# First tiles behind three norms made from the unnormed input, their results multiplied by the norm's factor

## The reference

```
def rms_norm(x, g):
    xf = x.astype(jnp.float32)
    y = xf * lax.rsqrt(jnp.mean(xf * xf, axis=-1, keepdims=True) + RMS_EPS)
    return (y * g.astype(jnp.float32)).astype(x.dtype)
...
        h = rms_norm(x, norm_mix_pre[l])
        u = h @ w_in[l]
...
        x = x + rms_norm(y, norm_mix_post[l])
        h = rms_norm(x, norm_ffn_pre[l])
        gu = causal_dwconv(h @ w_ffn_up[l], ffn_conv_w[l])
        g, up = jnp.split(gu, 2, axis=-1)
        y = (jax.nn.gelu(g, approximate=True) * up) @ w_ffn_down[l]
        x = x + rms_norm(y, norm_ffn_post[l])
...
        z = rmsnorm(h, g_mix[l]) @ w_in[l]
```

## Time and profile before

| | |
|---|---|
| median of 3 runs | 1609.29 us (1606.79 to 1611.38) |
| the profiled execution, its own time | 1603.75 us |
| its span, first to last instruction | 1602.0 us |
| PE busy | 1507.7 us, 94% |
| DVE busy | 1082.2 us, 68% |
| ACT busy | 825.8 us, 52% |
| POOL busy | 376.2 us, 23% |
| mean granted TensorE clock | 0.978 of full |

### The profile page before, as it was taken

The page is one execution under the profiler, slowest core; times in us unless marked ns, Lnnn a source line. Parts: engine busy times, 40 slices in busy tenths (PEclk is TensorE's granted clock), DMA queues, the critical chain, the costliest instruction groups (busy, mean ns, idle before and its releaser), DMA issues.

```text
span 1602.0 us, 32178 instructions
## 1 busy us (share of the span) xinstructions
PE 1507.7 (94%) x11588; PEld 1380.9 (86%) x11588; DVE 1082.2 (68%) x1790; ACT 825.8 (52%) x1426; POOL 376.2 (23%) x166
## 2 busy tenths in 40 slices
PE   5998879999789999889999999999999999999998
PEld 4976669999678989889999999999999888888886
DVE  3426457778568988674678997999998544454444
ACT  3335445555455422354466556776665444444444
POOL 1210112222112301012233234221212222222221
PEclk9998999999889999999999999999999999999999
DMA  6630226555324500054645555444444566666664
GB/s 237 234 109 25 66 67 183 180 186 183 106 81 143 164 10 28 15 169 161 184 145 171 182 184 182 148 133 142 138 138 131 183 185 184 194 185 186 184 192 144
DMA packets 66231, 234.86 MB, mean 147 GB/s; under 512 B 8200, under 2 KB 9240, under 8 KB 66160
## 3 DMA queue, kind: packets, MB, share of 16 engines
q1 hardware_dynamic: 65760, 232.31, 45.9%
q0 software_dynamic: 400, 1.59, 0.3%
HBM read 232.80 MB, written 1.06 MB: 146 GB/s over the span
## 4 chain that ended last, share of the span: by engine, by line
PE 72%; DVE 15%; ACT 6%; issue 5%; POOL 1%; DMA 1%; DVEq 0%; SPq 0%; ACTq 0%; POOLq 0%
PE psum L681 35%; PE psum L1372 22%; PE psum L1338 4%; DVE big L1611 3%; DVE w_lo L523 3%; ACT w_hi L509 2%; DVE big L1601 2%; PE psum L1031 2%; DVE big L1651 2%; PE psum L664 1%; ACT big L2187 1%; PE psum L981 1%; PE psum L739 1%; PE psum L1022 1%; PE psum L853 1%
## 5 line engine op out<-in xcount | busy, mean ns | idle before, releaser
L681 PE MATMUL psum<-x_hi,w_hi 128*128 128x256 f32 (+1 forms) x2152 | 624.9, 290 | 39.2 <-DVE x_lo L1427 13.2
L523 POOL TENSOR_TENSOR w_lo<-ring,w_hi 128x1024 fp32r<-128x1024 f32 x141 | 352.7, 2501 | 1117.0 <-ACT w_hi L509 1117.0
L681 PE MATMUL psum<-x_lo,w_hi 128*128 128x256 f32 (+1 forms) x2152 | 613.8, 285 | 0.0
L681 PE MATMUL psum<-x_hi,w_lo 128*128 128x256 f32 (+1 forms) x2152 | 610.3, 284 | 0.0
L509 ACT ACTIVATE w_hi<-ring 128x1024 fp32r<-128x1024 f32 x424 | 445.5, 1051 | 92.0 <-PE psum L681 71.6
L523 DVE TENSOR_TENSOR w_lo<-ring,w_hi 128x1024 fp32r<-128x1024 f32 x283 | 352.2, 1245 | 151.1 <-ACT w_hi L509 147.4
L681 PEld LDWEIGHTS psum<-x_hi,w_hi 128*128 128x128 f32 x2152 | 410.7, 191 | 49.2 <-issue 32.0
L681 PEld LDWEIGHTS psum<-x_hi,w_lo 128*128 128x128 f32 x2152 | 413.4, 192 | 0.0
L681 PEld LDWEIGHTS psum<-x_lo,w_hi 128*128 128x128 f32 x2152 | 411.4, 191 | 1.7 <-issue 1.4
L2095 DVE TENSOR_TENSOR h_lo<-big,h_hi 128x256 fp32r<-128x256 f32 x128 | 69.1, 541 | 163.0 <-ACT h_hi L2519 163.0
L1372 PE MATMUL psum<-w_lo,h_hi 128*128 128x512 f32 x512 | 161.0, 395 | 0.0
(11 more groups left out here) (315 smaller groups left out, 1738.0 us busy)
## 6 DMA issues: line engine op xcount, KB each, us to landing
ring<-experts SPq DMA_DIRECT2D x256, 512.0 KB, 3.5
ring<-w_ffn SPq DMA_DIRECT2D x66, 512.0 KB, 3.5
ring<-w_in SPq DMA_DIRECT2D x46, 512.0 KB, 3.6
ring<-w_mid SPq DMA_DIRECT2D x24, 512.0 KB, 3.5
ring<-w_out SPq DMA_DIRECT2D x16, 512.0 KB, 3.6
ring<-w_q SPq DMA_DIRECT2D x16, 512.0 KB, 3.9
big<-w_cmp SPq DMA_DIRECT2D x8, 512.0 KB, 5.1
big<-bias_rows POOLq DMA_DIRECT2D x1, 1536.0 KB, 9.2
```

The source lines that it names most:

```text
L523: eng.tensor_tensor(w_lo[:, n % RING, :], ring[:, n % RING, :], w_hi[:, n % RING, :].bitcast(F32), ALU.subtract).then_inc(low_ready2 if n ...
L681: mm = pe.matmul(dst, w[:, slot, k * P:(k + 1) * P], x[:, k, t0:t0 + width], start=(n == 0), stop=(n == 3 * len(chunks) - 1))
```

## The change

At each of the three places the first tiles (tile 0 of `w1_in`, two of the FFN, three of `w2_in`) are multiplied with the split of x times gain, without the norm's factor: `x_hi` and `x_lo` come straight from the residual (`raw_act` and `low_raw`), before the norm's sum is known. The factor comes later. At norm 0 all results of `w1_in` are multiplied by `rms` when they leave PSUM, and only the gates, which need the normed input itself, get it (8 DVE operations behind tile 11; `gate_logits` moves from behind tile 12 to behind tile 13). At norms 2 and 4 the results of the raw tiles are multiplied in PSUM (`scale_raw`), while the further tiles take the normed input as before: it is made and split beside the raw tiles, and written over `x_hi` and `x_lo` when PE is done with these (`tiles_used`). The sums of norms 0 and 3 are made from squares that DVE first adds in pairs (`fold_pair`), 4 matmuls in place of 8; those of norms 2 and 4 stand between the matmuls of the first raw tile. At the start the meta tokens and the `first` parameters are loaded behind the kept parameters and tile 0. `low_rank` moves one tile back, behind tiles 4 to 6. Loops of PE are written out in part. The diff, cut to its core:

```
-            sp.dma_start(hx[:, :, 0:N_META], meta_t).then_inc(meta_loaded, 16)
             sp.dma_start(kept_sb[:], kept).then_inc(param_loaded, 16)
-            sp.dma_start(first_sb, first).then_inc(first_loaded, 16)
-            sp.dma_start(oh_tab[0:32, :], rel).then_inc(rel_loaded, 16)
...
+
+            load_tile(w1_in, 0, 0)
+            sp.dma_start(first_sb, first).then_inc(first_loaded, 16)
+            sp.dma_start(oh_tab[0:32, :], rel).then_inc(rel_loaded, 16)
...
-                    for t in range(BODY):
+                    for t in range(1, BODY):
                         load_tile(src, t, t)
+                        if t == 2:
+                            sp.dma_start(hx[:, :, 0:N_META], meta_t).then_inc(meta_loaded, 16)
...
+            pool.wait_ge(neg_row, 1)
+            split_low(pool, 2, None, (2,))
...
-            def norm_pe(n, width, bank):
-                for k in range(KD):
+            def norm_pe(n, width, bank, rows=0):
+                for k in range(rows):
                     norm_row(n, k, width, bank)
+                for q in range(rows // 2, 4):
+                    pe.wait_ge(norm_folded, FOLDED[n] + q - rows // 2 + 1)
+                    mm = pe.matmul(psum[:, bank, 0:width], const("ones"), sq[:, 2 * q, 0:width], start=(q == 0), stop=(q == 3))
+                    if q == 3:
+                        mm.then_inc(norm_sums, 1)
...
+            def project_raw(slot, dst, width, r, norm=None):
+
+                n = 0
+                for k in range(KD):
+                    if norm is not None and k % 2 == 0:
+                        norm_row(norm[0], k, width, norm[1])
+                        norm_row(norm[0], k + 1, width, norm[1])
+                        pe.wait_ge(raw_split, 4 * r + k // 2 + 1)
+                    for w, x in ((w_hi, x_hi), (w_hi, x_lo), (w_lo, x_hi)):
+                        mm = pe.matmul(dst, w[:, slot, k * P:(k + 1) * P], x[:, k, 0:width], start=(n == 0), stop=(n == 23))
+                        n += 1
+                return mm
...
-            with pe.Fori(0, 2) as i:
-                for k in range(BODY):
-                    in1(k, i)
-            for k in range(2 * BODY, LATE):
+            project(tile_split(pe, B_IN1), psum[:, 0, 0:TX], TX, first=X_RAW0).then_inc(tiles_used, 1)
+            norm_pe(0, TX, 6)
+            bias_row()
+            for k in range(1, BODY):
                 in1(k)
-                if k == 12:
+            for k in range(BODY, LATE):
+                in1(k)
+                if k == 13:
...
-            norm_pe(2, TX, 0)
+            project_raw(tile_split(pe, B_FFN), psum[:, 0, 0:TX], TX, 0, (2, 2)).then_inc(tiles_used, 1)
+            project_raw(tile_split(pe, B_FFN + 1), psum[:, 1, 0:TX], TX, 0).then_inc(tiles_used, 1)
...
-            norm_pe(4, T2, 1)
+            project_raw(tile_split(pe, B_IN2), psum[:, 0, 0:T2], T2, 1, (4, 3)).then_inc(tiles_used, 1)
+            for s in (1, 2):
+                project_raw(tile_split(pe, B_IN2 + s), psum[:, s, 0:T2], T2, 1).then_inc(tiles_used, 1)
...
+            def fold_pair(n, q, width):
+                dve.wait_ge(norm_squares, KD * n + 2 * q + 2)
+                dve.tensor_tensor(sq[:, 2 * q, 0:width], sq[:, 2 * q, 0:width], sq[:, 2 * q + 1, 0:width],
+                                  ALU.add).then_inc(norm_folded, 1)
...
+            def low_raw(r, q, src, gain):
+                dve.wait_ge(raw_high, 4 * r + q + 1)
+                for k in (2 * q, 2 * q + 1):
+                    ins = dve.scalar_tensor_tensor(out=x_lo[:, k, 0:src.shape[2]], in0=src[:, k, :], scalar=colv(gain, k, k + 1),
+                                                   in1=x_hi[:, k, 0:src.shape[2]].bitcast(F32), op0=ALU.mult, op1=ALU.subtract)
+                ins.then_inc(raw_split, 1)
+
+            def scale_raw(tile, bank, width):
+                dve.wait_ge(tiles_used, tile + 1)
+                dve.tensor_tensor(psum[:, bank, 0:width], psum[:, bank, 0:width], rms[:, 0:width], ALU.mult).then_inc(raw_scaled, 1)
+
+            def norm_pair(q, src, width, gain):
+                for k in (2 * q, 2 * q + 1):
+                    ins = dve.scalar_tensor_tensor(out=sq[:, k, 0:width], in0=src[:, k, :], scalar=colv(gain, k, k + 1),
+                                                   in1=rms[:, 0:width], op0=ALU.mult, op1=ALU.mult)
+                ins.then_inc(norm_part, 1)
+
+            def low_pair(s, q, width):
+                dve.wait_ge(high_part, 4 * s + q + 1)
+                dve.tensor_tensor(x_lo[:, 2 * q:2 * q + 2, 0:width], sq[:, 2 * q:2 * q + 2, 0:width],
+                                  x_hi[:, 2 * q:2 * q + 2, 0:width].bitcast(F32), ALU.subtract).then_inc(x_split, 1)
...
+                    if behind is not None and q > 0:
+                        behind(q - 1)
+                if behind is not None:
+                    behind(3)
...
+            for q in range(4):
+                dve.wait_ge(high_part, 4 * X_RAW0 + q + 1)
+                for k in (2 * q, 2 * q + 1):
+                    ins = dve.scalar_tensor_tensor(out=x_lo[:, k, 0:TX], in0=hx1[:, k, :], scalar=colv("mix_pre", k, k + 1),
+                                                   in1=x_hi[:, k, 0:TX].bitcast(F32), op0=ALU.mult, op1=ALU.subtract)
+                ins.then_inc(x_split, 1)
+                if q == 1:
+                    split_low(dve, 0)
+            for q in range(4):
+                fold_pair(0, q, TX)
+            split_low(dve, 1)
+            norm_scale(0, TX, 6)
...
-                    dve.tensor_copy(z1[:, trip(k, i), :], psum[:, k % BODY, 0:TX]).then_inc(in1_even, 1)
+                dve.wait_ge(tiles_used, trip(B_IN1 + k + 1, i))
+                dve.tensor_tensor(z1[:, trip(k, i), :], psum[:, k % BODY, 0:TX], rms[:, 0:TX],
+                                  ALU.mult).then_inc((in1_even, in1_odd)[k % 2], 1)
...
+            for k in range(KD):
+                ins = dve.scalar_tensor_tensor(out=sq[:, k, 0:TX], in0=hx1[:, k, :], scalar=colv("mix_pre", k, k + 1),
+                                               in1=rms[:, 0:TX], op0=ALU.mult, op1=ALU.mult)
+                if k % 2:
+                    ins.then_inc(norm_part, 1)
...
-            norm_post(1, y1, lambda q: y1[:, 2 * q:2 * q + 2, :], TX, 4, "mix_post")
-            norm_pre(2, hx1, TX, 0, "ffn_pre")
-            low_norm(X_NORM2, TX)
+            norm_post(1, y1, lambda q: y1[:, 2 * q:2 * q + 2, :], TX, 4, "mix_post", lambda q: low_raw(0, q, hx1, "ffn_pre"))
+            split_low(dve, B_FFN + 2)
+            norm_scale(2, TX, 2)
+            norm_pair(0, hx1, TX, "ffn_pre")
+            norm_pair(1, hx1, TX, "ffn_pre")
+            scale_raw(B_FFN, 0, TX)
+            low_pair(X_NORM2, 0, TX)
+            norm_pair(2, hx1, TX, "ffn_pre")
+            low_pair(X_NORM2, 1, TX)
+            norm_pair(3, hx1, TX, "ffn_pre")
+            low_pair(X_NORM2, 2, TX)
+            low_pair(X_NORM2, 3, TX)
+            scale_raw(B_FFN + 1, 1, TX)
...
-            norm_post(3, y1, ffn_y, TX, 0, "ffn_post")
+            for q in range(4):
+                fold_pair(3, q, TX)
+            norm_post(3, y1, ffn_y, TX, 0, "ffn_post", lambda q: low_raw(1, q, hx, "mix2"))
             dve.tensor_scalar(stay, colv("mu"), -1.0, 1.0, ALU.mult, ALU.add)
 
-            norm_pre(4, hx, T2, 1, "mix2")
-            low_norm(X_NORM4, T2)
...
             low(2)
+            norm_scale(4, T2, 3)
+            scale_raw(B_IN2, 0, T2)
+            norm_pair(0, hx, T2, "mix2")
             shift(0)
-            low(3)
+            scale_raw(B_IN2 + 1, 1, T2)
+            norm_pair(1, hx, T2, "mix2")
             shift(1)
+            norm_pair(2, hx, T2, "mix2")
+            norm_pair(3, hx, T2, "mix2")
+            for q in range(4):
+                low_pair(X_NORM4, q, T2)
             low(4)
+            scale_raw(B_IN2 + 2, 2, T2)
             shift(2)
             low(5)
             shift(3)
+            low(6)
+            shift(4)
             dve.wait_ge(up_ready, 4)
             step(dve.tensor_scalar(logdec, logdec, -float(np.exp(-0.5)), None, ALU.mult))
-            low(6)
-            shift(4)
...
+            def raw_act(r, src, gain, ready):
+
+                for q in range(4):
+                    ready(q)
+                    for k in (2 * q, 2 * q + 1):
+                        ins = act.activation(x_hi[:, k, 0:src.shape[2]], src[:, k, :], ACT.Copy, scale=colv(gain, k, k + 1))
+                    ins.then_inc(raw_high, 1)
+                    act.activation(sq[:, 2 * q:2 * q + 2, 0:src.shape[2]], src[:, 2 * q:2 * q + 2], ACT.Square).then_inc(norm_squares, 2)
...
+            for k in range(KD):
+                ins = act.activation(x_hi[:, k, 0:TX], hx1[:, k, :], ACT.Copy, scale=colv("mix_pre", k, k + 1))
+                if k % 2:
+                    ins.then_inc(high_part, 1)
+                if k == 3:
+                    split_high(act, 0)
             norm_act(hx1, TX, lambda q: act.wait_ge(x_loaded, 16))
```

(31 more changed lines are left out.)

104 lines of the change are left out of this document (57 added, 47 removed).

## The result

| | before | after |
|---|---|---|
| median of 4 runs each, same chip | 1608.04 us (1604.76 to 1611.38) | 1588.59 us (1585.69 to 1591.46) |
| ratio of the times, 95% interval | | 0.9883 (0.9859 to 0.9906) |
| the profiled execution, its own time | 1603.75 us | 1587.87 us |
| its span | 1602.0 us | 1586.1 us |
| DVE busy | 1082.2 us | 1102.2 us |

The ratio is a gain of 18.8 us on 1608 (15.1 to 22.7); the two profiled executions differ by 15.9 us. The forecast was 13.1 us. Faster was right, and the time, 1588.6 us, lies 0.6 us inside the lower end of the range (1588 to 1603).

A forecast was written before the change was run, and what follows sets the result against it. PE was taken to bound the kernel, losing idle time and then a half-speed tile at norms 0, 2 and 4. 8.8 - 2.6 + 6.9 = 13.1 us off 1609.3 gave 1596.2 us, range 1588 to 1603.

The forecast's parts named there:

- Place 1: Start of the kernel, norm 0 and `w1_in`: tile 0 at 13.0 us, tile 1 at 21.1 instead of 29.9; gain 8.8 us.
- The step with the parameters: Start: ACT waits for the kept parameters, taken to land at 8.2 us (bounds 8.7 and 7.6).
- Four chunks of `x_hi`, to 10.6: Start: ACT makes raw `x_hi` at 0.28 us a chunk (bounds 0 and 0.43), done at 10.6 us.
- Place 2: FFN's entry at norm 2: down tile 1.0 us later plus 1.6 us for a low clock; loss 2.6 us.
- PE has been idle for 3.6 us: FFN's entry: PE idle between tile 35's end at 237.6 us and the first down tile at about 241.2.
- the 1.6 us charged for the clock: FFN's entry: cost of a lower clock after PE's idle time ahead of the down tile, between 0 and 2.35 us.
- The block by POOL's split: FFN's entry: DVE's normed chunks, with two SBUF inputs, stand still during POOL's split of tile 35; 1.7 us lost.
- the chain from the scaling of tile 33 to the split of the down tile: FFN's entry: copies, convolution, gelu, `h_lo` and splits take 7.7 us, before 6.5, as the gelu's table load loses its cover.
- Place 3: `w_in` of layer 2, norms 3 and 4: raw tiles and folded squares; gain 6.9 us, bounds 4.5 and 8.5.
- its first rival: "Ports and clock do less": FFN's entry costs nothing, layer 2's gives 8; 16 to 19 us, 1592 us; chance 0.15.

The follow-up runs named there:

- the nine new starts: Traces of kernels with the changed start and folded squares, against the kernel before; norm 1's reciprocal starts at 203.1 us on the mean, against 210.9.
- the undone kernel: Changed kernel without the raw FFN tiles 32 and 33: 1595.03 us; where layer 2 is discussed, without the raw tiles of `w2_in`: 1596.93 us.
- Layer 2's entry undone: Changed kernel without the three raw tiles of `w2_in`, norm 3's folded squares kept: 1596.93 us, ratio to before 0.9947.

## The experiments: the FFN's entry, where the forecast was wrong

**Early grants.** The two `sem_inc` that tiles 34 and 35 wait for stand right behind norm 2's reciprocal. The mean ahead of it is the last reader of the bank that tile 34 needs.
```diff
             norm_scale(2, TX, 2)
+            dve.sem_inc(ffn_conv_g, 2)
+            dve.sem_inc(ffn_conv_u, 2)
...
             scale_raw(B_FFN + 1, 1, TX)
-            dve.sem_inc(ffn_conv_g, 2)
-            dve.sem_inc(ffn_conv_u, 2)
```


> The changed kernel with the two grants that tile 34 and 35 wait for (ffn_conv_g and ffn_conv_u) given right behind norm 2's reciprocal, ahead of the scalings and the splits of x_lo. Theory (the wait that the forecast overlooked: PE stood until DVE had come to its grants): with reference to norm 1's reciprocal of the same trace, tile 34 starts 3 us earlier, near +19.2 us instead of +22.3 us, its idle time 3.9 us instead of 7.0 and ended by x_lo; the first down tile then waits for its own weights' split on DVE and starts only 0.3 to 0.8 us earlier. The forecast's own sum: PE idles a second time ahead of the down tile, the clock falls, and the down tile comes 1 us later than in the changed kernel and runs at half speed for 1.6 us more.

PE in order of time, and then stretches (us, busy us and count of PE, PEld, DVE, ACT and POOL, granted clock, DMA share, GB/s), the second of them behind the last wait for `h_lo`:
```profile
222.20 0.55 PE L697 MATMUL psum<-x_hi,w_hi 128*128 128x256 f32 x1 [3.32 <-DVE x_lo L1494]
...
232.65 0.58 PE L724 MATMUL psum<-h_hi,w_hi 128*128 128x256 f32 x1 [3.06 <-DVE w_lo L529]
...
236.86 0.28 PE L697 MATMUL psum<-x_hi,w_hi 128*128 128x256 f32 x1
...
409.86 0.36 PE L724 MATMUL psum<-h_hi,w_hi 128*128 128x256 f32 x1 [1.90 <-DVE h_lo L1708]
```
```profile
232.00:237.00 5.00, 4.35 (x26) 4.35 (x27) 4.89 (x7) 2.37 (x4) 2.02 (x1) 0.66 0.55 129
410.00:414.00 4.00, 2.93 (x24) 2.72 (x24) 1.19 (x2) 0.98 (x3) 0.00 (x0) 1.00 0.74 208
```
For comparison, PE in the second trace of the changed kernel:
```profile
226.31 0.55 PE L697 MATMUL psum<-x_hi,w_hi 128*128 128x256 f32 x1 [6.19 <-DVEq L1677]
...
233.89 0.39 PE L724 MATMUL psum<-h_hi,w_hi 128*128 128x256 f32 x1
...
236.84 0.28 PE L697 MATMUL psum<-x_hi,w_hi 128*128 128x256 f32 x1
```
The run has the shape that the forecast drew for the change itself: tile 34 on the first low pair, a second idle stretch of 3.06 us ahead of the down tile, and the down tile in part at half speed (4.21 us long, 2.83 in the changed kernel). Its place differs less than expected. Counted from N the down tile starts at 30.24 us, against 30.68 in the first trace of the changed kernel and 30.24 in the second; the theory's 0.3 to 0.8 us is met against the first trace alone. The tile behind it starts at 34.45, against 33.51 and 33.19: 0.9 to 1.3 us later, which is the part of the forecast's loss that the late grant kept away.

What neither expected is that N to D is 1.0 us shorter all the same. From that tile behind the first down tile to D all the other kernels take 174.9 to 175.2 us, this one 173.0. Some 1.0 us of that is inside the loop, where a pair of steps takes 17.09 us instead of 17.22 and `h_lo` is ready 3.8 us ahead of its down tile instead of 2.8; 0.9 us is the last wait for `h_lo` (1.90 instead of 2.82). Why the loop has two such rhythms is not settled.

**Early grants and early scaling.** Also `scale_raw(B_FFN + 1, 1, TX)` straight behind `scale_raw(B_FFN, 0, TX)`.

> As the kernel with the early grants, and the scaling of tile 33's result moved from the end of DVE's list to right behind that of tile 32, so that the chain to the first down tile starts near 222 instead of 225.6 us. Theory (with the grant early, that chain sets the down tile): the down tile 1 to 2 us earlier than in the changed kernel, as far as PE's tiles 34 and 35 at half speed (2 x 5.2 us behind +19.5) let it. Rival (ScalarE, which must first make the four high pairs, holds the chain): no earlier than with the early grant alone.

ACT in order of time, its first work on the chain to the down tile:
```profile
226.80 0.84 ACT L2380 ACTIVATE big<-psum,big 128x256 f32<-128x256 f32 x2 [0.84 <-DVE big L1686]
```
The down tile starts at 30.23 from N, where it did with the early grants alone (30.24). The rival's result holds, but not its reason: ACT was done with the four high pairs and idle for 0.84 us, until DVE's copy of the taps (L1686), which stands behind all the low pairs. That copy ends 23.6 us behind N in both kernels, so the moved scaling gained nothing. N to D is 208.32, so the gain of the run before is gone too.

**Late POOL split.** POOL waits for both scalings before it splits tile 35; nothing else moves.
```diff
-            pool_splits(3, B_IN2 + 2)
+            pool_splits(3, B_FFN + 3)
+            pool.wait_ge(raw_scaled, 2)
+            pool_splits(B_FFN + 3, B_IN2 + 2)
```


> The changed kernel, but GpSimd starts its split of tile 35 only when both results are scaled, behind DVE's normed chunks and low pairs; nothing else moves. Theory (VectorE's operations with two SBUF inputs stand still while GpSimd's subtract runs): the four normed chunks take 1.7 us instead of 3.0, tile 34 starts 1.3 us earlier counted from norm 1's reciprocal, the down tile too. Rival (the longer operations wait for something else, or the block only moves on): the chunks still show a 1.7 us one, or another DVE operation does, and tile 34 starts within 0.4 us of where it did.

DVE, PE and POOL in order of time:
```profile
220.56 1.67 DVE L1490 SCALAR_TENSOR_TENSOR sq<-hx,kept_sb,rms 128x256 f32<-128x256 f32 x4
...
227.76 1.91 DVE L1697 SCALAR_TENSOR_TENSOR big<-psum,big 128x255 f32<-128x255 f32 x4 [0.62 <-ACT big L2383]
```
```profile
226.18 0.55 PE L699 MATMUL psum<-x_hi,w_hi 128*128 128x256 f32 x1 [5.64 <-DVEq L1679]
...
233.76 0.38 PE L726 MATMUL psum<-h_hi,w_hi 128*128 128x256 f32 x1
...
411.80 0.55 PE L726 MATMUL psum<-h_hi,w_hi 128*128 128x256 f32 x1 [2.82 <-DVE h_lo L1711]
```
```profile
227.31 2.38 POOL L529 TENSOR_TENSOR w_lo<-ring,w_hi 128x1024 fp32r<-128x1024 f32 x1 [26.97 <-DVE psum L1486]
```
The theory holds to the tenth for the chunks and for tile 34: the four normed chunks take 1.67 us instead of 3.02, and tile 34 starts 20.93 us behind N instead of 22.29. POOL's split now lies beside the convolutions, whose one input is in PSUM, and they take 1.91 us as before. The down tile comes 2.2 us earlier counted from N, 0.9 more than the theory had for it, and N to D is 1.9 us shorter. The Trainium skill (SBUF — State Buffer, Who interferes with whom) says that a VectorE instruction with two SBUF inputs contends with a GpSimd one that reads SBUF, and that one with at most one, outside the two-port modes, does not. Both halves agree with the rows: 3.02 us beside the split and 1.67 without it for the chunks, 1.91 either way for the convolutions. At the end little of it is left: N lay late in this trace (205.25), and the last down tile, behind the same wait of 2.8 us, ran at half speed, so D to K took 64.40 us.

**Early grants, late POOL split.** Both edits; POOL waits for the last low pair instead of the scalings (`pool.wait_ge(x_split, 4 * X_NORM2 + 4)`).

> The changed kernel with the early grants, and GpSimd's split of tile 35 held until DVE has made the last low pair of norm 2. Theory (both effects add, since the one moves PE's start and the other the chain): counted from norm 1's reciprocal tile 34 starts near +18.5 us (changed kernel +22.3), the down tile near +28.9 (+30.7), norm 3's reciprocal at +213.5 to +215.5 (+217.3); the whole 2 to 3 us shorter than the changed kernel, 1585 to 1587. Rival (the steps of the FFN's loop are set by something else, so that what is gained at its entry is lost there): the down tile comes 1.8 us earlier but norm 3's reciprocal at +216.5 or later.

Tile 34 starts 18.28 us behind N and the down tile 28.74, both as the theory said, and N to D is 206.84, 1.6 us shorter than changed; norm 3's reciprocal is at +215.49. But the two effects do not add beyond the entry, as the theory had it: the pair takes no more off N to D than the late split alone, and the whole is not 2 to 3 us shorter. The median, 1588.57 us, ratio 0.9896 (0.9879 to 0.9912), is that of the changed kernel: this version is better by its trace at this place, and cannot be told from the changed one by its time.

**FFN's entry as before, with early grants.**
```diff
             norm_pre(2, hx1, TX, 0, "ffn_pre")
-            low_norm(X_NORM2, TX)
             dve.sem_inc(ffn_conv_g, 2)
             dve.sem_inc(ffn_conv_u, 2)
+            low_norm(X_NORM2, TX)
```


> The kernel with the FFN's entry as before (no raw tiles 32 and 33), but its two grants given behind norm 2's chunks, ahead of the low pairs. Theory (in the kernel before, too, PE stood for the grants and not for its input): the first FFN tile starts at the first low pair, about 2 us earlier counted from norm 1's reciprocal (+14.2 us instead of +16.25), and the first down tile likewise 1.5 to 2 us earlier; so the grant alone is worth more than the raw tiles' 0.4 us, and norm 1's reciprocal to norm 3's takes 215.5 to 216.5 us instead of 217.8. Rival: the first tile runs at half speed for longer and the down tile waits for its split: under 0.5 us.

PE in order of time:
```profile
219.17 0.55 PE L697 MATMUL psum<-x_hi,w_hi 128*128 128x256 f32 x1 [6.74 <-DVE x_lo L1466]
...
233.83 0.38 PE L724 MATMUL psum<-h_hi,w_hi 128*128 128x256 f32 x1 [0.63 <-DVE w_lo L529]
```
The theory fell, and the rival's "under 0.5 us" holds, though for another cause. The tile starts 16.17 us behind N, as without the edit (16.25), now released by `x_lo`. In the kernel before, grant and first low pair came within 0.1 us of each other, since DVE made all eight normed chunks first; the wait on the grant in the earlier trace rows hid nothing. It became 3 us long only in the changed order, in which the chunks and the pairs alternate and the grants stand behind the last.

## The experiments: how much is scatter

> The kernel before, unchanged, for a second trace of it. Theory (where the low clock falls differs between executions and moves identical code by 1 to 3 us): norm 1's reciprocal, the last down tiles and the end differ from the first trace by 1 to 3 us, by steps in the attention and between 570 and 750 us. Rival (the clock follows the program alone): all landmarks within 0.3 us of the first trace.

The second trace of before has N 2.5 us later, D 1.6 us and K 1.1 us; its end is 4.8 us later (span 1606.8). The rival fell; the theory holds for the three landmarks, and the end differs by more than its 3 us.

> The changed kernel, unchanged, for a second trace and more times. Theory (the three places are worth 7.7, 0.4 and 7.0 us by the traces made so far, 15 in all, and the rest of the first result's 18.8 us is where the low clock fell in stretches that the change does not touch): the gain is 14 to 18 us by the medians, and from norm 1's reciprocal on the intervals up to the reciprocal at the head of layer 2's chunk loop repeat to 0.3 us, while the stretch behind it, 190.8 us in the first trace, comes out at 192 to 194. Rival (the change itself shortens layer 2's later part too): 190.8 us again, and 18 us or more.

The gain by the medians is 16.2 us, by the ratio 0.9902 (0.9887 to 0.9917) 13.3 to 18.2. From K to the end it took 1114.2 us, not 1112.0, and the stretch in layer 2 that took 190.8 us (from K to the next reciprocal on `rms`, at 664.87 in the first trace) came out at 193.65: the rival fell. In the two traces of before it takes 193.2 and 194.0 us, so the 190.8 of the first trace is no part of the gain. One part of the theory failed: D to K is 1.7 us shorter than in the first trace, not within 0.3. Its last down tile ran at full clock, the first trace's at 0.59. The same stretch of the two, busy times and clock as above:
```profile
412.00:416.00 4.00, 3.82 (x20) 3.62 (x19) 0.83 (x1) 0.08 (x1) 0.00 (x0) 0.59 0.68 235
```
```profile
412.00:416.00 4.00, 3.02 (x24) 2.82 (x24) 1.47 (x2) 1.17 (x3) 0.00 (x0) 1.00 0.52 178
```
Behind one and the same wait of 2.8 us the clock fell at once (late POOL split: from D to norm 3's reciprocal 9.77 us), in the course of the tile (8.9 us in six kernels), or not at all (7.4 us in this one and that with the early scaling).

## Why the prediction was right, and where it was wrong

**Place 1, "gain 8.8 us": right, 1 us too large at N.** The step with the parameters held (landed by 8.07, forecast 8.2). "Four chunks of `x_hi`, to 10.6" was mis-sized: 0.42 us a chunk, so 11.1, the upper bound that the text gave. Tile 0 then started at 13.38 (13.0). Tile 1 started at 21.77 in this trace and between 20.3 and 21.8, at 21.1 on the mean, in the nine new starts, which is the forecast's figure; in the three old ones it lies at 29.7, 30.1 and 30.9. That is 9.1 us on the means. At N 7.8 us of it are left. The rest went between tile 1 and N, a stretch that scatters by 3.5 us among the new starts, and its cause stays open. PE waited for no weight tile's landing; the only waits up to 60 us are 0.38 us for POOL's split and 0.23 us for the normed chunks ahead of `gate_logits`, for which the text allowed 0.5. The bias table took 12.8 us to land instead of 9.2 and delayed nothing that PE waited for.

**Place 2, "together a loss of 2.6 us": wrong, it changed almost nothing.** The columns give a gain of 0.2 us, the undone kernel one of 0.5, and the second trace of before lies 0.3 to 0.5 us below the changed ones, so that not even the sign is shown; no trace comes near a loss of 2.6. The step that failed is that PE makes tile 34 on the first `x_lo` pair. It took the release of that tile for its input and did not ask for its second condition, the grant behind DVE's whole list, though the earlier trace rows name it. With the grant late, PE started tile 34 3.0 us after that pair and ran on to the down tile, so "PE has been idle for 3.6 us" and the 1.6 us charged for the clock did not come about. The run with early grants shows this: tile 34 then starts on the pair, and the second idle stretch (3.06 us) and a down tile 1.4 us too long appear.

But the grant is the smaller part of the miss. With early grants the tile behind the down tile starts 34.45 us behind N, 0.9 to 1.3 us later than in the changed kernel and 0.7 later than in the first trace of before (33.73), not 2.6. The other 1.9 us come in the main from two sizes. The block by POOL's split cost 1.35 us, not 1.7 (late POOL split); so a scalar_tensor_tensor is not exempt, which the forecast had to leave open. And the chain from the scaling of tile 33 to the split of the down tile took 6.6 us (225.99 to 232.62), not 7.7: the gelu's table load lay under the convolutions after all. These make 1.4 of the 2.0 us by which the down tile's weights were ready before the time forecast; the other 0.6 is not traced.

**Place 3, "6.9 us": right, 1.5 us too small against the mean.** 8.4 us by the columns. Norm 4's mean, the wait behind tile 100 (2.76 us, forecast 3), its release by `x_lo` and the block of DVE (1.87 us for two chunks that take 0.87 elsewhere: 1.0, forecast 1.2) came as described. Tile 102 was done at 450.5, 39.3 us behind D; the forecast, moved to the same D, had 40.3. Layer 2's entry undone gives 5.9 us for the raw tiles, and the forecast's was 5.8. The rest is in what it was measured against: with 1.1 us taken off for the folding, the two traces of before still lay 1.3 and 0.9 us above the undone kernel at this place. In the second of them the 0.9 lies in the last down tile, at a granted clock of 0.50 over its first 4 us, where the undone kernel had 0.58. So the mechanism and the size stand.

**The sum.** 7.8 + 0.2 + 8.4 = 16.4 us by the traces, 18.8 and 16.2 us by the two pairs of medians. Of the 3.3 us between 13.1 and 16.4, Place 2 makes +2.8, Place 3 +1.5 and Place 1 -1.0. The gain lies above the 9 to 16 us to which the text gave 0.66, in the 16 to 19 us of its first rival (0.15), and the time fell just inside the range. So the total is partly luck: one of its three terms was off by 2.8 us, and an error the other way in Place 1 hid a part of that. The most likely single number should have been near that of the rival "ports and clock do less", but for a reason that it did not contain: the port did block and the clock did fall; PE was late for another cause, and the chain was shorter.

**What the profile should show.** Met: tile 0 at 13, tile 1 at 21, `x_lo` ending the wait of 3 us behind tile 100, no wait for a landing between 25 and 40, in1's results without a wait; tile 101 ended some 7 us earlier counted from D (forecast 6). Not met: the wait behind tile 33 was 7.0 us and ended at the grant, the first down tile came 0.1 us earlier counted from N (30.68 against 30.79), and at full speed. L1488 beside POOL's split took 3.02 us for four chunks where 1.67 is its undisturbed time.

## What to carry to other kernels

An instruction waits for all of its conditions; where a row names one releaser, list the others and ask which is next when you move the first, above all grants that stand at the end of another engine's list. Here an earlier grant moved the tile by 2.5 us and the down tile behind it by 0 to 0.4, and it bought a second idle stretch and a slow clock: see what the next wait is before you count such a gain. When parts are worth a few us each, cut the traces at common instructions and compare pieces, with more than one trace of each kernel; a kernel's end carries 4 us of scatter from code that nobody touched. And keep a split on GpSimd away from the VectorE operations with two SBUF inputs that PE waits for: moved by 7.5 us, the split gave 1.9 us from N to D for one wait in POOL's list.

## What was not expected of the hardware

The granted clock is not the same in two executions of one program: behind the same wait of 2.8 us ahead of the last down tile it was 1.00 over the next 4 us in one trace of the changed kernel and 0.59 in the other, which is 1.5 us. PE can be continuously busy and still have the lower level: where PE was busy for the whole 5 us, the grant was 0.50 between 115 and 120 us in the changed kernel and 0.66 between 125 and 130 us in the kernel before. Just ahead of the first, PE had been idle only for 0.36 us (at 114.79), between short matmuls.

For the one code stretch from K to the end, 14 traces took 1111.6 to 1116.2 us. What part of that is the clock was not separated. Nor was the cause found of the two rhythms of the FFN's loop.
